# Reordering the score of the first event, and the weighting against the weight splits on GpSimd, in a hybrid decoder layer

## The reference

```python
z = jnp.einsum("bhqd,bhkd->bhqk", q_blk, k).astype(jnp.float32) * scale
causal = key_pos[None, :] < q_pos[:, None]
log_beta = jax.nn.log_sigmoid(z)
log_keep = jnp.where(causal, jax.nn.log_sigmoid(-z), 0.0)
suffix = lax.cumsum(log_keep, axis=3, reverse=True) - log_keep
w = jnp.where(causal, jnp.exp(log_beta + suffix), 0.0)
return jnp.einsum("bhqk,bhkd->bhqd", w.astype(v.dtype), v)
```

## Time and profile before

| | |
|---|---|
| median of 3 runs | 3526.72 us (3525.69 to 3530.97) |
| the profiled execution | 3525.69 us, span 3524.0 us |
| mean granted clock of PE | 0.917 of full |
| PE matmuls busy | 2965.2 us (84%) |
| PE weight loads busy | 2402.9 us (68%) |
| DVE / ACT / POOL busy | 1647.1 / 944.6 / 1392.9 us |
| DMA | 328.35 MB, mean 93 GB/s |

### The profile page before, as it was taken

How to read it: one execution, slowest core, us unless ns; L and a number is a source line. 1 busy time by engine, 2 the same in 40 slices (tenths; PEclk the granted TensorE clock), 3 DMA queues, 4 the chain that set the end, 5 groups by cost and what they waited for, 6 DMA issues and landing times. The chain is left out here.

```text
span 3524.0 us, 37070 instructions
## 1 busy us (share of the span) xinstructions
PE 2965.2 (84%) x13484; PEld 2402.9 (68%) x13484; DVE 1647.1 (47%) x1611; ACT 944.6 (27%) x1470; POOL 1392.9 (40%) x696
## 2 busy tenths in 40 slices
PE   6599899999999877777675554999976799999998
PEld 5488688888888655555564443778765678787876
DVE  0310066666666587878786564332313412222123
ACT  3200044444444333333332332111113100001011
POOL 4134355444454354545553001444420334344431
PEclk9799999999999889888888777999987899999998
DMA  4243433433333112122122444333213111111112
GB/s 130 87 143 137 113 92 119 120 114 108 102 102 114 69 58 75 61 70 69 62 70 90 150 184 173 120 107 130 78 48 137 60 48 48 42 48 42 48 48 113
DMA packets 133368, 328.35 MB, mean 93 GB/s; under 512 B 13089, under 2 KB 59809, under 8 KB 133281
## 3 DMA queue, kind: packets, MB, share of 16 engines
q1 hardware_dynamic: 133280, 327.20, 28.2%
HBM read 232.78 MB, written 94.37 MB: 93 GB/s over the span
## 5 line engine op out<-in xcount | busy, mean ns | idle before, releaser
L172 POOL TENSOR_TENSOR ff_wh<-ff_w,one 128x1024 fp32r<-128x1024 f32 x64 | 121.2, 1893 | 509.7 <-PE ff_ps L194 416.8
L522 PE MATMUL sb_psg<-uh,sb_wh 128*128 128x512 f32 x768 | 306.9, 400 | 13.8 <-POOL sb_wl L669 13.8
L683 POOL TENSOR_TENSOR sb_beta<-sb_beta,sb_rest 128x128 f32<-128x128 f32 (+7 forms) x128 | 164.0, 1281 | 380.7 <-DVE sb_rest L739 380.7
L522 PE MATMUL sb_psg<-uh,sb_wl 128*128 128x512 f32 x768 | 313.2, 408 | 0.0
L522 PE MATMUL sb_psg<-ul,sb_wh 128*128 128x512 f32 x768 | 306.7, 399 | 0.0
L172 POOL TENSOR_TENSOR mg_wh<-mg_w,one 128x1024 fp32r<-128x1024 f32 x32 | 62.5, 1954 | 475.6 <-DMA mg_w<-in_w_branch 305.6
L1518 PE MATMUL mg_ps<-mg_yh,mg_wh 128*128 128x512 f32 x512 | 204.3, 399 | 52.9 <-POOL mg_wl L179 32.2
L739 DVE TENSOR_TENSOR_SCAN sb_rest<-sb_rest 128x128 f32<-128x128 f32 (+7 forms) x128 | 181.4, 1417 | 138.3 <-ACT sb_rest L631 137.5
L932 PE MATMUL ssd_psg<-uh,sg_wh 128*128 128x512 f32 x384 | 179.0, 466 | 60.7 <-ACT ssd_out L971 60.7
L194 PE MATMUL ff_ps<-ff_fh,ff_wh 128*128 128x512 f32 x512 | 203.4, 397 | 27.4 <-DVE ff_fl L1738 27.4
L194 PE MATMUL ff_ps<-vh,ff_wh 128*128 128x512 f32 x512 | 200.3, 391 | 13.6 <-POOL ff_wl L179 13.6
(11 more groups left out here) (284 smaller groups left out, 7629.6 us busy)
## 6 DMA issues: line engine op xcount, KB each, us to landing
sb_w<-in_w_in SPq DMA_DIRECT2D x48, 512.0 KB, 5.0
scratch_proj<-sb_out SPq DMA_DIRECT2D x48, 512.0 KB, 3.0
sb_k<-scratch_qk SPq DMA_DIRECT2D x64, 256.0 KB, 6.3
mg_raw<-scratch_y SPq DMA_DIRECT2D x32, 512.0 KB, 5.8
mg_w<-in_w_branch SPq DMA_DIRECT2D x32, 512.0 KB, 4.4
mg_gate<-scratch_proj SPq DMA_DIRECT2D x32, 512.0 KB, 3.3
ff_w<-in_w_up SPq DMA_DIRECT2D x32, 512.0 KB, 3.6
ff_w<-in_w_down SPq DMA_DIRECT2D x32, 512.0 KB, 3.6
```

The source lines that it names most:

```text
L172: nc.gpsimd.tensor_tensor(ring.hi[:, s].rearrange("p k n -> p (k n)"), ring.raw[:, s], ring.ones[:].broadcast_to([P, D]), ALU.mult).then_i ...
L522: last = nc.tensor.matmul(ps_g[:, h], l[:, s, k], r[:, k, h * HALF:(h + 1) * HALF], start=(k == 0 and j == 0), stop=(k == KB - 1 and j == 2))
L683: nc.gpsimd.tensor_tensor(beta[:, i % 3, 0:cols], beta[:, i % 3, 0:cols], rest[:, i % 3, 0:cols], ALU.mult).then_inc(weighted, 1)
```

## The change

PE's list: in event 0 the score now comes ahead of the projection, as in all other events, and the 11 matmuls of event 0 come in two portions like the others. POOL's list: in every iteration the weighting comes first, and the round and the rest that stand in that iteration come behind it.

```diff
             for i in range(EVENTS):
-                if i == 0:
-                    project(0, fill_from[1])
                 if i < N:
                     score(i)
                 if i >= Y_LAG and (i - Y_LAG) % 4 == 3:
                     weigh_values(i - Y_LAG)
-                middle = (fill_from[i] + fill_from[i + 1]) // 2 if i < N else 0
-                if 0 < i < N:
+                if i < N:
+                    middle = (fill_from[i] + fill_from[i + 1]) // 2
                     project(fill_from[i], middle)
                 if LAG <= i < N + LAG:
                     pe.wait_ge(weighted, i - LAG + 1)
                 for u in at_event[i]:
                     turn(u)
-                if 0 < i < N:
+                if i < N:
                     project(middle, fill_from[i + 1])
...
             for i in range(N):
                 cols = (i % TB + 1) * P
+                pool.wait_ge(scanned, i + 1)
+                pool.wait_ge(beta_done, i + 1)
+                nc.gpsimd.tensor_tensor(beta[:, i % 3, 0:cols], beta[:, i % 3, 0:cols], rest[:, i % 3, 0:cols],
+                                        ALU.mult).then_inc(weighted, 1)
                 for m in range(1, FILL):
                     if i == max(0, begins(m) - 2):
                         round_block(m)
                     if i == max(0, begins(m) - 2) + 1:
                         rest_of_block(m)
-                pool.wait_ge(scanned, i + 1)
-                pool.wait_ge(beta_done, i + 1)
-                nc.gpsimd.tensor_tensor(beta[:, i % 3, 0:cols], beta[:, i % 3, 0:cols], rest[:, i % 3, 0:cols],
-                                        ALU.mult).then_inc(weighted, 1)
```

## The result

The changed kernel takes 3583.79 us in the median (3583.15 to 3585.86, 4 runs) against 3526.99 us of the kernel before beside it. The ratio is 1.0163, with an interval of 1.015 to 1.0176: 57 us, 1.6% slower. The forecast was 3572 us in a range of 3547 to 3597.

The account below looks back on a forecast made before the run. PE was taken to set the stage's pace; waits 42.2, restarting 1, clock 3 and start -0.5 gave 45.7 us on 3525.69, so 3571.4, forecast as a 3572 us median, range 3547 to 3597.

Parts of the forecast that it names:

- What bounds the stage: Stick-breaking stage: PE, busy 763.3 of 775.0 us, sets the pace and never waits for a weighting product of POOL.
- Which splits come late: POOL's rests behind the weighting: late for blocks of remainder 3, 0 and 2 by 6, 23 places; other remainders in time.
- The size of the waits: PE's waits for late rests: 42.2 us in 23 places, plus 1 us for restarting.
- Who goes first: When the weighting ends, DVE's waiting operation goes ahead of POOL's rest, which loses 1.0 us each time.
- The rival in which POOL goes first: At the end of the weighting POOL precedes DVE; late waits stay 22.9 us, 3550 us in all; chance 0.14.
- The clock: PE's clock falling after fifteen waits of 2.3 to 2.8 us: a quarter times 1.6 us is 6, taken as 3.
- That rival, in which it falls every time: PE's clock falls after every one of 15 waits, 24 us instead of 3, 3593 us in all; chance 0.13.
- the prediction's own last sign: Prediction is wrong if matmul spacings of 0.43 us follow most of PE's waits for the rest.
- The start: Event 0, score before projection on PE: -0.5 us, bounds -3.5 to +3.4.
- The reading of the last k piece: Event 0: the last piece of q and k lands at 433.2 us, 8.9 us after issue, and the score needs it.
- The rounds: POOL's rounds move behind weighting b-2, a whole event ahead of need, so they have room.

Follow-up runs that it names:

- e9: Kernel before, neither edit, with a pair's eight values turned four each in events 4 and 5 instead of eight in event 4: 3520.48 us, ratio 0.9975.
- e4: Kernel before with only POOL's rest moved behind the weighting, the round kept ahead, PE's event 0 as before: 3585.25 us, ratio 1.0158.
- e6: Changed kernel plus a DVE wait for the rest at 23 places, so POOL goes first: 3557.16 us, ratio 1.0082.
- e5: Changed kernel plus eight matmuls ahead of PE's wait for the split of blocks 3, 6, ..., 45: 3568.72 us, ratio 1.0114.
- e3: Kernel before with only POOL's round moved behind the weighting, the rest kept ahead, PE's event 0 as before: 3535.84 us, ratio 1.0021.
- e2: Kernel before with only the edit of POOL's list, PE's event 0 as before: 3586.3 us, ratio 1.0166.
- e7: Changed kernel with the rest of only blocks 3, 6, ..., 45 ahead of the weighting again: 3537.59 us, ratio 1.0026.
- e8: Changed kernel with every block's rest in the same iteration as its round, behind the weighting of iteration b-2: 3536.94 us, ratio 1.0021.

## Why the prediction was right

- **What bounds the stage** held. PE sets the pace, and no wait for a weighting shows on it in any trace. e9 is the same rule from the other side: eight waits of 1.0 us taken away gave 8 us.
- **Which splits come late** held: 23 waits, in threes per 16 events, at blocks of remainder 2, 3 and 0 by 6; the other 24 blocks none. e4 shows that the rests alone do it.
- **The size of the waits** was a little too high. The step had 42.2 us and 1 us for restarting; the trace has 39.6 from start to start. That these 3.6 us took back part of what the clock added was luck.
- **Who goes first** held. DVE's waiting operation went ahead of the rest, which took 3.32 us instead of 2.40: 0.9, where the earlier trace rows gave 1.0. The rival in which POOL goes first (3550) is ruled out for this kernel, and e6, which forces it, lands at 3557; its 15 waits, 22.4 us from start to start, are near the rival's 22.9. By the Trainium skill (SBUF — State Buffer, "SBUF: two separate sides") the pair is held by one of the two for a whole instruction; the rows agree, and add that the waiting DVE operation took it before POOL's next one.
- **The clock** is the step that was mis-sized. The sum had 3 us, from a fall after one in four gaps of 2.8 us in the next stage, marked down because these waits are shorter. It was 18.8 us: after 11 of 15 waits of 2.03 to 2.50 us the clock fell. The nearer evidence was the fall behind the one wait of 1.88 us in this very stage, which the prediction named only for its rival. That rival, in which it falls every time (3593), was nearer for this term. e5 shows the cost by itself. In e6 the 15 waits are 1.1 to 1.5 us and it never fell, but there the waits are shorter as well. The 15.8 us that this term lacked, less the 3.6 above and with 0.5 for the start, make 12.7 us, against 12 between 3572 and 3584. By the prediction's own last sign, spacings of 0.43 us behind most of the waits, it was close to wrong: they follow 11 of the 23 waits, but 11 of the 15 long ones.
- **The start** was forecast at -0.5, and the traces give 0.0 once they are counted from the same issue. The reading of the last k piece held: the score began 12.06 us after the first issue of q (434.53), where 433.2 would be 11.98. But the low clock lasted 4.2 us from there and not 3.6.
- **The rounds** were costed at nothing. In the changed kernel nothing shows, but alone (e3) they cost 8 us. What makes them free there, that the rest moves behind the weighting with them, was not named.
- **Left open:** why four of the 15 long waits were not followed by a fall. Length alone does not decide it. In the three traces with 15 long waits each (the changed kernel, e2, e4) the clock fell behind all 21 waits at blocks of remainder 0, and behind 12 of the 24 at blocks of remainder 3. Blocks 3, 15 and 39 had no fall in any of the three, though block 15 waits 2.43 to 2.45 us and falls came after 2.03 us elsewhere. That the profiled executions differ by 61.6 us and the medians by 57 is mostly explained: 1.25 us are the later start and 2.7 the tail, neither of them the change's.

## What to carry to other kernels

Where one engine sets the pace, as here, ask of every moved instruction only when its result is needed there, and compare that with the end of whatever it now stands behind. The rest cost nothing while it filled POOL's idle time before the scan; behind the weighting it hung on the whole chain. Ask it also of what is pushed along: in e3 the moved round did no harm, the unmoved rest behind it did. Price a new wait of TensorE of 2 us or more with the clock behind it, here 1.7 us in 11 of 15 cases, and look at what the other engine does at the same moment: GpSimd's 2.4 us became 3.3.

## What the runs showed of the hardware that was not expected

- Waits of PE of 2.03 to 2.50 us in an otherwise busy stretch were followed by 3.4 us at 1.2 GHz in 11 of 15 cases, in the changed kernel and again in 11 of 15 in e2 and in e4, at the same blocks but for 21 and 27. With 1.1 to 1.5 us (15 waits of e6), or with eight matmuls put into them (e5), there was none. The moment of the fall is not fixed to the wait: at block 9 the clock was still full 1 us after PE had resumed at 587.48 us, at block 24 it was at 1.2 GHz when PE resumed at 845.38.
- Two waits of 1.38 and 1.57 us at the stage's end, 2.64 us apart, were followed by full clock in the kernel before, e2, e3, e5, e6 and e7, and by half in the changed kernel, e4 and e8, 2.7 us in the stage's length. It goes with none of the edits.
- A GpSimd operation that is already running holds up a VectorE scan of 1024 columns. The rest of 2.40 us began 0.5 us ahead of the scan, which took 4.05 us instead of 2.29 (e3).
